# Side work at other steps, row-half pairs of scores, joined gate weights and column-shaped row sums in a two-block fp32 transformer kernel

## The reference

```
# first block, per layer
proj = rms_norm(x) @ w_in                                # 2048 -> 5952
o_a = dense attention, 8 heads, rope and norm on q, k     # "A"
o_b = dense attention from low-rank projections, 4 heads  # "B"
o_c = neighbourhood attention with a bias table, 4 heads  # "C"
x = x + rms_norm(concat(o_a, o_b, o_c) * silu(gates) @ w_out)

# second block, per layer
mod = silu(c) @ w_mod + b_mod                            # one row of 3 * 2048
h = rms_norm(x) * (1 + scale) + shift
a_q, a_k, a_v, s_u, s_v, c_q, c_k, c_v, c_g, z = split(h @ w_in)
y_a = sliding-window attention, 16 heads of 64, 4 kv heads
y_b = gelu(s_u) * (causal spatial mixing of norm(gelu(s_v)))
y_c = gated linear attention with gates log_sigmoid(c_g @ w_gate_up + b)
x = x + gate * rms_norm((concat(y_a, y_b, y_c) * silu(z)) @ w_out)
```

## Time and profile before

| | |
|---|---|
| median of 3 runs | 3762.35 us (3760.0 to 3763.01) |
| profiled execution | 3766.83 us, its span 3765.1 us |
| TensorE busy | 3553.3 us, 94% of the span |
| VectorE, ScalarE, GpSimd busy | 1718.8, 1141.5, 1139.8 us |
| mean granted TensorE clock | 0.975 |

### The profile page before, as it was taken

How to read it: one execution, slowest core, us unless ns; L and a number is a source line. 1 busy time by engine, 2 the same in 40 slices (tenths; PEclk the granted TensorE clock), 3 DMA queues, 4 the chain that set the end, 5 groups by cost and what they waited for, 6 DMA issues and landing times.

```text
span 3765.1 us, 52278 instructions
## 1 busy us (share of the span) xinstructions
PE 3553.3 (94%) x17005; PEld 2819.4 (75%) x17005; DVE 1718.8 (46%) x2884; ACT 1141.5 (30%) x1918; POOL 1139.8 (30%) x1242
## 2 busy tenths in 40 slices
PE   6999999999799999999997999999997999999998
PEld 5767777778686677777786778877786878877786
DVE  4533476443444236654425335544535334545533
ACT  3122333322321333332323234322323224322221
POOL 5664776560175477765300000012000000002000
PEclk9999999999899999999998999999998999999999
DMA  7444444453354354434432311322433322321332
GB/s 248 127 118 128 141 138 118 120 180 112 131 175 118 88 160 141 137 112 148 158 99 101 95 57 57 95 59 65 159 101 109 96 61 57 95 65 52 122 135 100
DMA packets 184717, 430.87 MB, mean 114 GB/s; under 512 B 21238, under 2 KB 26257, under 8 KB 178328
## 3 DMA queue, kind: packets, MB, share of 16 engines
q1 hardware_dynamic: 146344, 292.60, 24.7%
q0 software_dynamic: 33472, 109.06, 10.3%
q10 hardware_dynamic: 4656, 26.07, 1.8%
HBM read 406.58 MB, written 24.75 MB: 115 GB/s over the span
## 4 chain that ended last, share of the span: by engine, by line
PE 89%; DVE 5%; issue 3%; ACT 1%; DMA 1%; DVEq 0%; ACTq 0%; SPq 0%; POOL 0%; POOLq 0%
PE bank L699 22%; PE bank L701 21%; PE bank L700 21%; PE bank L772 4%; PE bank L792 3%; PE bank L758 2%; PE bank L878 2%; PE bank L694 2%; PE bank L781 2%; PE bank L696 1%; PE bank L695 1%; PE bank L718 1%; PE bank L899 1%; PE bank L1031 1%; PE bank L950 1%
## 5 line engine op out<-in xcount | busy, mean ns | idle before, releaser
L699 PE MATMUL bank<-wlo,act_hi 128*128 128x512 f32 (+1 forms) x3712 | 1531.8, 413 | 1.5 <-DVE zone L1530 0.9
L701 PE MATMUL bank<-whi,act_lo 128*128 128x512 f32 (+1 forms) x3712 | 1448.0, 390 | 0.0
L700 PE MATMUL bank<-whi,act_hi 128*128 128x512 f32 (+1 forms) x3712 | 1446.6, 390 | 0.0
L1475 DVE TENSOR_TENSOR wlo<-stage,whi 128x1024 fp32r<-128x1024 f32 (+1 forms) x496 | 670.0, 1357 | 730.1 <-ACT whi L1116 718.2
L699 PEld LDWEIGHTS bank<-wlo,act_hi 128*128 128x128 f32 x3712 | 704.1, 190 | 205.8 <-issue 63.2
L700 PEld LDWEIGHTS bank<-whi,act_hi 128*128 128x128 f32 x3712 | 704.7, 190 | 153.4 <-issue 24.7
L701 PEld LDWEIGHTS bank<-whi,act_lo 128*128 128x128 f32 x3712 | 702.5, 189 | 149.1
L1116 ACT ACTIVATE whi<-stage 128x1024 fp32r<-128x1024 f32 (+1 forms) x496 | 514.0, 1044 | 779.7 <-PE bank L701 381.6
L2291 POOL TENSOR_TENSOR macc<-macc,mprod 128x512 f32<-128x512 f32 x360 | 497.5, 1382 | 66.5 <-POOL mprod L2284 66.5
L2284 POOL TENSOR_SCALAR mprod<-wmod,csil 128x512 f32<-128x512 f32 x384 | 310.2, 808 | 296.6 <-PE bank L815 192.8
L2328 POOL DMA_DIRECT2D macc<-in_gla_w_gate_up x2 | 1.1, 542 | 1189.2 <-DVE Y L1948 1189.2
(11 more groups left out here) (255 smaller groups left out, 3244.0 us busy)
## 6 DMA issues: line engine op xcount, KB each, us to landing
stage<-in_w_in SPq DMA_DIRECT2D x352, 512.0 KB, 3.7
wmod<-in_w_mod POOLq DMA_DIRECT2D x384, 256.0 KB, 3.1
stage<-in_w_out SPq DMA_DIRECT2D x128, 512.0 KB, 3.8
out<-Y ACTq DMA_DIRECT2D x20, 1024.0 KB, 5.0
zone<-out SPq DMA_DIRECT2D x4, 4096.0 KB, 14.9
stage<-in_w_in SPq DMA_DIRECT2D x16, 320.0 KB, 3.7
Y<-in_x SPq DMA_DIRECT2D x4, 1024.0 KB, 10.2
rpb_tiles<-rpb_pad POOLq DMA_DIRECT2D x16, 224.0 KB, 4.9
```

The costliest lines, as they stand in the source:

```text
L699: pe.matmul(out, hi_x, lo_w, start=(k == 0), stop=False)
L700: pe.matmul(out, hi_x, hi_w, start=False, stop=False)
L701: mm = pe.matmul(out, lo_x, hi_w, start=False, stop=(k == KC - 1))
L1475: dve.tensor_tensor(wlo[:, j % RH, :, 0:width], stage[:, j % RS, :, 0:width], whi[:, j % RH, :, 0:width].bitcast(F32), ALU.subtract).then_ ...
```

## The change

1. **Steps.** `UNIT_PV` goes from 3 to 4. Units stand at successive steps, but not where the step or its `pv` falls on local steps 0 and 1 or 4 and 5 of a panel (`unit_steps`); A's units follow their query job (`AQ_JOBS`). Jobs of B stand three steps later or so, A's key job at 117 instead of 112 (its norm starts at 107 instead of 106), A's query jobs from 124 on instead of 122. The level turns skip local steps 15 and 0.
2. **Scores in pairs.** `head_of` and `units_of` are changed so that duos d and d + 1 are two heads in the lower and the upper half of the partitions. Both are scored at the first one's step, the halves by turns.
3. **c_g weights joined.** The high and the low part lie side by side, so one product gives both: 32 products of 32 and 16 columns. c_g lies in 32 rows, and the gate weights are loaded twice.
4. **Row sums turned.** `macc` is the stationary operand in four parts, the ones the moving one; the sums lie in a column each, are copied as 128 x 4 and written as 512 single floats.

```
 U_B, U_C, U_A = 0, 16, 32
+UNIT_TURN, UNIT_PV, ROW_SUM = 2, 4, 4
+def unit_steps(first, n):
+    free = [s for s in range(first, first + 2 * n) if (s + UNIT_PV) % KC not in (ROW_SUM, ROW_SUM + 1)]
+    return free[:n]
+AQ_JOBS = (124, 131, 136, 141, 148, 153, 158, 165)
-for first, steps in ((U_B, [48, *range(51, 64), 64, 67]), (U_C, [*range(83, 97), 99, 100]),
...
+for first, steps in ((U_B, unit_steps(50, 16)), (U_C, unit_steps(83, 16))):
+for h in range(A_H):
+    UNIT_AT.update({s: U_A + 4 * h + i for i, s in enumerate(unit_steps(AQ_JOBS[h] + 1, 4))})
-UNIT_TURN, UNIT_PV = 2, 3
-                     (J_VB, (42, 43, 44, 45)), (J_AK, (112, 113)), (J_AQ, (122, 127, 134, 139, 144, 151, 156, 161))):
+                     (J_VB, (43, 44, 44, 45)), (J_AK, (117, 118)), (J_AQ, AQ_JOBS)):
-CQ_AT, QROPE_AT, CKV_AT = 17, 28, 32
+CQ_AT, QROPE_AT, CKV_AT = 17, 31, 35
-A_LOAD_AT, AK_AT, AQ_AT = 105, 106, (114, 130)
+A_LOAD_AT, AK_AT, AQ_AT = 105, 107, (116, 131)
-LEVEL_AT = 74
+LEVEL = [s for s in range(74, 120) if s % KC not in (KC - 1, 0)][:4 * (LEVELS + 1) + 1]
...
         def head_of(d):
             g = d // 4
-            return 8 * (g // 4) + g % 4 + 4 * (d % 4 // 2)
+            return 8 * (g // 4) + g % 4 + 4 * (d % 2)
...
-            for n in (2 * (d % 2), 2 * (d % 2) + 1):
+            for n in (2 * (d % 4 // 2), 2 * (d % 4 // 2) + 1):
...
         JOB_CG = [(w, x) for k in range(KC) for w, x in
-                  ((cgw_hi[:, k, :], act_lo[:, k, :]), (cgw_hi[:, k, :], act_hi[:, k, :]),
-                   (cgw_lo[:, k, :], act_hi[:, k, :]))]
+                  ((cgw_r[:, k, :], act_hi[:, k, :]), (cgw_r[:, k, 0:G_RANK], act_lo[:, k, :]))]
...
-                pe.matmul(MSUM[0:1, :], ones[:, 0:1], macc[:, p % 2, :], start=True, stop=True).then_inc(mod_sum.sem, 1)
+                for i in range(PW // P):
+                    mm = pe.matmul(MSUM[:, i:i + 1], macc[:, p % 2, tok(i)], ones[:, 0:1], start=True, stop=True)
+                mm.then_inc(mod_sum.sem, 1)
...
             def swa_scores(l, d):
...
                 if d >= 2:
-                    pe.wait_ge(exp_done.sem, exp_done.at(1, l, d - 1))
-                for n, ks, cols_ in units_of(d):
-                    mm = pe.matmul(bank[4 + d % 2][:, cols_], qT_s[half, g % 2, tok(n)],
-                                   kT_s[half, g // 4, ks[0] * P:(ks[-1] + 1) * P], start=True, stop=True)
+                    pe.wait_ge(exp_done.sem, exp_done.at(1, l, d))
+                for i in range(2):
+                    for e in range(2):
+                        n, ks, cols_ = units_of(d + e)[i]
+                        half = slice(e * S_D, (e + 1) * S_D)
+                        mm = pe.matmul(bank[4 + e][:, cols_], qT_s[half, g % 2, tok(n)],
+                                       kT_s[half, g // 4, ks[0] * P:(ks[-1] + 1) * P], start=True, stop=True)
...
-                if s in DUO_AT:
+                if s in DUO_AT and DUO_AT[s] % 2 == 0:
                     swa_scores(l, DUO_AT[s])
...
-                act.dma_start(mod_dram[bass.ds(l, 1), bass.ds(p * PW, PW)], mrow[:, :]).then_inc(mod_row.sem, 16)
+                act.dma_start(mod_dram[bass.ds(l, 1), bass.ds(p * PW, PW)].rearrange("o (i c) -> c (o i)", c=P), mrow[:, :],
+                              allow_slow_non_contiguous=True).then_inc(mod_row.sem, 16)
```

56 lines of the change are left out of this document (27 added, 29 removed).

## The result

The changed kernel took **3691.84 us** (median of 4 runs, 3689.26 to 3696.48), the kernel before 3761.18 (4 runs, 3759.04 to 3763.01). The ratio is 0.9817, with a 95% interval of 0.9800 to 0.9834, so 62 to 75 us less. Predicted were 3682 us, with a range from 3652 to 3712. The time lies inside, in part by luck: what follows shows that two parts of the sum, the new order of block 1 and the row sums, were wrong by some 19 and 13 us in opposite directions.

A forecast was written before the change was run, and what follows sets the result against it. TensorE, busy for 94% of the span, was taken to bound the kernel. The terms summed to -80.2 us, taken from the median of 3762.35 to give 3682 us, with an 8 in 10 range of 3652 to 3712.

The forecast's parts named there:

- Paired scores: Score groups on TensorE: a pair costs about what one duo did, with 32 fewer group edges; -34.6 us, bounds -14 to -37.
- the rival's case (no overlap): Paired score groups: two heads' scores run one after the other, so 29.8 us are not won: 3712 us; chance 0.08.
- c_g: Joined c_g weights: 32 products instead of 48 at 0.232 us each; -7.4 us for two layers.
- Level turns: Ends of panels 7 and 8, block 2: waits for ScalarE and mask, and the slow clock, go; -28 us, bounds -20 and -30.
- Row sums: 24 turned row sums on TensorE, each shorter by 0.24 us; -5.8 us, bounds 0 and -8.
- this is hidden: Write of 512 single floats after each row sum: next sum 16 steps away, final reader far behind, so no cost.
- The rival that I had drawn from the write: Row sums' write: single floats hold ScalarE's queue, 3802 us if each issue held it 8 us; chance 0.04.
- A's keys: Block 1: moving the key job five steps later removes its rope wait, 5 of 9 us per layer counted; -10 us, bounds -3 and -18.
- its own sign of being wrong: Listed under what would show the prediction wrong: waits of the dense matmuls for low weights; no size given.
- Panel ends 3, 5 and 7: Block 1: `pv` at local step 15 no longer waits 1.2 us for `take_turn`; -6.4 us, bounds -3 and -8.
- Gate panels: Panels 8 and 9, block 1: second `pv` waits 5.2 us for `finish` behind the gate; +13 us, bounds 0 and +20.
- First jobs of B: The latent norm's own job moves three steps away from its wait, -2 us; the `QPT` wait stays, 0.

The follow-up runs named there:

- experiment 1: The kernel before with the paired scores as its only change: 3726.17 us, ratio 0.9912 to the kernel before.
- experiment 3: The changed kernel with all eight passes of a pair in the lower 64 rows, the upper heads' scores not computed: 3717.59 us.
- experiment 2: The changed kernel with a pair's passes issued one half first, then the other, instead of by turns: 3687.41 us.
- experiment 4: The changed kernel with the level turns on consecutive steps from 74 on, as before: 3717.92 us.
- experiment 5: The changed kernel with the row sums and their write as before (one row, one contiguous write): 3710.44 us.
- experiment 6: The changed kernel with each partition's four floats written to neighbouring places, 128 pieces of 16 bytes instead of 512 of 4: 3710.19 us.
- experiment 7: The changed kernel with GpSimd starting its seventh round of the modulation only after VectorE's key rope of the layer: 3686.58 us.
- experiment 10: The changed kernel with all step numbers of block 1 (units, jobs, ropes, distance to the PV product) as before: 3686.82 us.

## Why the prediction was right, and where it was not

- **Paired scores**, -34.6: measured -31.9 (experiment 1). The groups themselves give 30.3 where 29.8 were predicted. The edges, put at 4.8, gave 1.6 of what was won; the waits for ScalarE in front of transposes and scores come to 3.1 us (L900 1.3, L876 1.1, L890 0.7), where there were 0.6 before, though the prediction took no new wait. The reason was right, and the rival's case (no overlap) is what experiment 3 built, at 26 us where the rival had 30. The prediction read the overlap from level rows in which the halves alternate; experiment 2 shows that they need not.
- **c_g**, -7.4: measured -3.71 per layer, exact. For the second load of gate weights panel 6 is 0.8 and 0.7 us longer, with +1 predicted in all; that panel differs by 0.6 between profiles of kernels without the second load.
- **Level turns**, -28: measured -26.7 by the panels and 26 to 28 by experiment 4.
- **Row sums**, -5.8: the passes and the copy give -5.5. (The prediction's two figures, 0.10 and 0.1 us, add up to 0.20 per sum and not to the 0.24 that it multiplied; measured are 0.22 to 0.27.) But the term "this is hidden" of the write was wrong: 512 single floats delay the weight loads, GpSimd gets slower, and VectorE, which is what TensorE waits for in panels 7 and 8, gets faster. Experiments 5 and 6 put that at some 13 us to the good. The rival that I had drawn from the write looked at ScalarE's queue alone (0.4 us measured, so it fell), not at who shares the DMA engines.
- **A's keys**, -10: the step that failed. The key job's wait of 7.4 us, a loss of 9.1 with the clock, went. But 3.1 and 6.2 us came back for the low weights in front of step 116 and 6.5 and 2.2 at the query job: 9.6 and 8.4 per layer. The prediction named both places as "late next" and priced them at 4 per layer. Panel 7 is 5.4 and 6.6 us shorter, but 3.6 of that is less work and some 1.4 its own end, so that 0.4 and 1.6 are left for the keys. With the old sums (experiment 5) the term has the other sign: there the same places lose 16 and 13 us. The prediction took the length of VectorE's chain as given, whereas more than a quarter of it was GpSimd beside it (experiment 7). Waits of dense products for low weights were its own sign of being wrong, and they came.
- **Panel ends 3, 5 and 7**, -6.4: losses of 1.34 to 1.38 us each became 0.33, 0.63 and 0: -6.3.
- **Gate panels**, +13: `pv` waits for `finish` behind the gate, just as described (timeline above). The waits were predicted at 5.2 us and are 5.0 to 6.8; they lose 7.0 to 8.7 with the lower clock behind them. The ends of panels 8 and 9 lost some 20 us for both layers before, with the clock, and lose some 33 now: the term was right in size. That panels 8 to 11 together are 19 us longer is more than this only because some 6 us of work moved in.
- **First jobs of B**, -2: panels 0 to 2 are 1.5 and 3.5 us shorter, with 0.5 of that from two row sums; they vary by 2 to 3 us between profiles. The waits at step 135, put at 0, lost some 4 us and now lose 1 to 2 at 137 (1 to 5 in the other profiles of the same order).

In sum: block 2 came out nearly as predicted (-69 predicted with the gate weights, -65 measured). In block 1 I had -11 with the row sums; the panels give -5, in a block whose length differs by 12 us between profiles of the same order. In the order of work alone the error is larger, since experiment 5 (new order, old sums) stands at 3710 and block 2 alone would give 3761 - 65 = 3696: the new order costs some 14 us with the old sums, where I had -5. Block 1 in the profiles says the same: 1996 us there, against 1980 and 1976 in the kernel before and in experiment 1. The 13 us of the slowed GpSimd hid that, and I had not foreseen them: that the time came within 10 us of the forecast is luck to that extent. With an uncertainty of some 6 us on each of these, the signs stand and the sizes are rough. In the old order the new row sums are worth some 9 us by the same reckoning (3696 against 3687 in experiment 10), of which 5.5 are direct; why the slowed GpSimd gives less there stays open.

## What to carry over

When a step number is moved away from a wait, ask which engine's chain was late, how long that chain is and what stretches it: here the wait moved twice along VectorE's chain, and only with GpSimd off VectorE's side and the query sums earlier did it leave panel 7. When work moves from one panel to another, take it out of the panels' times before reading them as waits. A DMA's cost is not only its issue and its landing, but also what it does to the loads beside it, and through them to the pace of an engine off the critical path. Small products in separate halves of TensorE's rows are worth issuing together; in this kernel either order did.

## What the hardware showed that I had not expected

- Passes in the lower and in the upper 64 rows run beside each other even when four passes of one half stand ahead of the other half's in the program: the first of each start 13 ns apart, and the group is as short as with halves by turns (30.9 against 30.7 us for 32).
- A write of 512 single floats from 128 partitions takes ScalarE 0.40 us to issue and lands in 5.8 us. By the packets in the trace, averaged over stretches of 2 us behind all 24 writes, 4096-byte packets on GpSimd's queue that start 4 to 8 us behind the issue take 1.1 to 1.5 us each instead of 0.23, and the 2048-byte packets of the weight stream up to 0.7 instead of 0.1. With 128 pieces of 16 bytes (landing 2.3 us) nothing of the kind is seen.
- VectorE's subtraction of two 128x1024 tiles takes 1.22 us with GpSimd idle or multiplying a tile by one number per partition, and 1.72 on average beside GpSimd's additions of two tiles; five other traces agree (1.22 to 1.24 and 1.76 to 1.80).
- A kernel can get faster by slowing an engine's supply: with the single floats GpSimd waits 181 us more for its weights (and 109 less for TensorE), and the whole is 13 us shorter than the direct saving explains.
